# Test operations on paired words and on every second word of a bank, placed ahead of the first matmul

## What is computed

```python
h = rmsnorm(x, norm_g)
proj = jnp.einsum('bld,dn->bln', h, w_in)            # first layer, 18432 columns
...
ya = jnp.einsum('blc,cd->bld', ya * jax.nn.silu(za), w_out_a)
yb = jax.nn.gelu(s5_scan(u, a_re, a_im, log_dt, b_re, b_im, c_re, c_im, d_skip))
...
return x + jnp.einsum('bld,de->ble', m, w_o)
...
mod = cond @ w_ada[l] + b_ada[l]                     # second layer
h = rms_norm(x, norm_g[l]) * (1.0 + scale[:, None, :]) + shift[:, None, :]
z = h @ w_in[l]
...
y = jnp.concatenate([y_a, y_b], axis=-1) @ w_out[l]
x = x + gate[:, None, :] * y
return rms_norm(x, final_g)
```

## Time and profile before

| | us |
|---|---|
| median of 3 runs | 2667.97 |
| lowest and highest run | 2667.52, 2670.11 |
| the profiled execution's own time | 2670.03 |
| its span, first to last instruction | 2668.8 |

### The profile page before, as it was taken

The page is one execution under the profiler, slowest core; times in us unless marked ns, Lnnn a source line. Parts: engine busy times, 40 slices in busy tenths (PEclk is TensorE's granted clock), DMA queues, the critical chain, the costliest instruction groups (busy, mean ns, idle before and its releaser), DMA issues.

```text
span 2668.8 us, 30016 instructions
## 1 busy us (share of the span) xinstructions
PE 2631.5 (99%) x11928; PEld 2159.8 (81%) x11928; DVE 1638.4 (61%) x2187; ACT 845.1 (32%) x1139; POOL 390.9 (15%) x295
## 2 busy tenths in 40 slices
PE   9989999999999999999999999999999999999997
PEld 7878888888888888888888888877888888888786
DVE  6678888787887765445444775556465563234434
ACT  5122222222222222222322332332565563233321
POOL 0034343433443421000000000010000000000001
PEclk9999999999999999999999999989999999999999
DMA  5233333333333333667555675623222222322333
GB/s 184 96 112 112 105 114 99 121 110 104 116 103 125 128 121 120 215 202 245 186 193 192 207 240 181 197 95 129 95 80 73 86 80 87 111 95 87 115 122 111
DMA packets 119867, 353.07 MB, mean 132 GB/s; under 512 B 15408, under 2 KB 22832, under 8 KB 119728
## 3 DMA queue, kind: packets, MB, share of 16 engines
q1 hardware_dynamic: 119728, 351.16, 39.7%
HBM read 321.68 MB, written 23.07 MB: 129 GB/s over the span
## 4 chain that ended last, share of the span: by engine, by line
PE 96%; DVE 2%; issue 1%; POOL 0%; ACT 0%; DMA 0%; SPq 0%; DVEq 0%; POOLq 0%; ACTq 0%
PE bank L512 29%; PE bank L513 28%; PE bank L514 28%; PE bank L678 2%; PE bank L680 2%; PE bank L679 2%; PE bank L721 1%; PE bank L711 1%; PE bank L576 1%; PE bank L564 1%; DVE X L1814 0%; PE bank L704 0%; PE bank L702 0%; PE bank L502 0%; DMA W<-in_w 0%
## 5 line engine op out<-in xcount | busy, mean ns | idle before, releaser
L1138 DVE TENSOR_TENSOR WL<-W,WH 128x1024 fp32r<-128x1024 f32 (+1 forms) x456 | 592.2, 1301 | 528.3 <-ACT WH L816 527.0
L816 ACT ACTIVATE WH<-W 128x1024 fp32r<-128x1024 f32 (+1 forms) x456 | 480.6, 1056 | 1008.6 <-PE bank L514 768.8
L512 PE MATMUL bank<-hH,WH 128*128 128x512 f32 x1792 | 700.3, 391 | 10.7 <-DVE WL L1138 6.8
L513 PE MATMUL bank<-hL,WH 128*128 128x512 f32 x1792 | 699.1, 390 | 0.0
L514 PE MATMUL bank<-hH,WL 128*128 128x512 f32 x1792 | 698.8, 390 | 0.0
L512 PEld LDWEIGHTS bank<-hH,WH 128*128 128x128 f32 x1792 | 337.1, 188 | 89.9 <-DVE WL L1138 7.2
L514 PEld LDWEIGHTS bank<-hH,WL 128*128 128x128 f32 x1792 | 337.1, 188 | 70.6
L513 PEld LDWEIGHTS bank<-hL,WH 128*128 128x128 f32 x1792 | 337.2, 188 | 70.2
L512 PE MATMUL bank<-h2H,WH 128*128 128x512 f32 x640 | 252.6, 395 | 0.1
L514 PE MATMUL bank<-h2H,WL 128*128 128x512 f32 x640 | 249.4, 390 | 0.0
L513 PE MATMUL bank<-h2L,WH 128*128 128x512 f32 x640 | 249.1, 389 | 0.0
(11 more groups left out here) (260 smaller groups left out, 3604.5 us busy)
## 6 DMA issues: line engine op xcount, KB each, us to landing
W<-in_w SPq DMA_DIRECT2D x335, 512.0 KB, 3.7
W<-in_ada SPq DMA_DIRECT2D x96, 512.0 KB, 4.4
W<-in_wa SPq DMA_DIRECT2D x32, 512.0 KB, 3.9
W<-in_wo SPq DMA_DIRECT2D x32, 512.0 KB, 3.9
W<-in_wvv SPq DMA_DIRECT2D x32, 512.0 KB, 3.7
W<-in_wb SPq DMA_DIRECT2D x16, 512.0 KB, 3.7
URAW<-U SPq DMA_DIRECT2D x96, 64.0 KB, 3.1
scr_am<-SO SPq DMA_DIRECT2D x16, 256.0 KB, 2.0
```

Source lines behind the costliest of these rows:

```text
L512: e.matmul(o, wh, xh, start=first, stop=False)
L513: e.matmul(o, wh, xl, start=False, stop=False)
L816: e.activation(WH[:, n % NB, c], W[:, i % NW, c], ACT.Copy).then_inc(sem["hi"], 1)
L1138: e.tensor_tensor(WL[:, s, c], W[:, plan.item_of[n] % NW, c], WH[:, s, c].bitcast(F32), ALU.subtract).then_inc(sem["lo_v"], 1)
```

## The change

At the head of the program test operations are put in, whose results nothing reads. The 12 warm-up matmuls go.

GpSimd first fills four tiles with 0.5: `TM` (128x2048 words), `TW` (128x128), `TQ` and `TD[0]` (128x512 each). They lie in memory that is not in use at this time. TensorE waits for `const` and for the second and third of these signals, runs 14 matmuls of 512 columns in fp32r into banks 7 and 6, signals, and then runs 42 + 8 + 6 + 9 further ones in fp32r and 3 + 3 + 8 in f32, nearly all with a moving operand whose words are read in another order, and one on `IDT`, all into bank 5. When the 14 are through, VectorE runs 27 operations of 512 words on bank 7 and on `TD`, and ScalarE 18 of 256 words on bank 6 and on `TD[0]`; both wait after each for its own signal. VectorE's `keep_u(0)`, which writes over the test tiles for the first time, waits for the last test matmul and for ScalarE's tests.

```diff
+    TM, TW = at("TM", 164, [128, 2048], F32R), at("TW", 172, [128, 128], F32R)
+    TQ = at("TQ", 172.5, [128, 512])
+    TD = [at(f"TD{i}", 174.5 + 2 * i, [128, 512]) for i in range(2)]
+    TR = at("TR", 178.5, [128, 256], F32R)
...
         e.wait_ge(*nth("const", 4))
-        for _ in range(WARM):
-            e.matmul(bank[7][:, 0:128], IDT[:, :], IDT[:, :], start=True, stop=True)
+        e.wait_ge(*nth("test", 2))
+        for i in range(14):
+            mm = e.matmul(bank[7 - i % 2][:, :], TW[:, :], TM[:, 0:512], start=True, stop=True)
+        mm.then_inc(sem["test"], 1)
+        x = TM[:, 0:512]
+        two = x.rearrange("p (a b) -> p b a", a=2)
+        for m in (two,
+                  x.rearrange("p (b a) -> p b a", a=2),
+                  x.rearrange("p (a b) -> p b a", a=4),
+                  x.rearrange("p (c a b) -> p c b a", a=2, b=16),
+                  x.rearrange("p (c a b) -> p c b a", a=2, b=128),
+                  TM[:, :].rearrange("p (a b) -> p b a", a=2)[:, 0:256, :],
+                  x.rearrange("p (c a b) -> p c b a", a=4, b=64)):
+            for i in range(6):
+                e.matmul(bank[5][:, :], TW[:, :], m, start=True, stop=True)
+        for i in range(8):
+            e.matmul(bank[5][:, 0:256], TW[:, :], TM[:, 0:256].rearrange("p (a b) -> p b a", a=2), start=True, stop=True)
+        for i in range(6):
+            e.matmul(bank[5][:, :], TW[0:64, :], two[0:64], start=True, stop=True)
+        for i in range(9):
+            e.matmul(bank[5][:, :], TW[:, :], two, start=i == 0, stop=i == 8)
+        for i in range(3):
+            e.matmul(bank[5][:, :], TQ[:, 0:128], TQ[:, :], start=True, stop=True)
+        for i in range(3):
+            e.matmul(bank[5][:, :], TQ[:, 0:128], TQ[:, :].rearrange("p (a b) -> p b a", a=2), start=True, stop=True)
+        for m in (TQ[:, :], TQ[:, :].rearrange("p (a b) -> p b a", a=2)):
+            for i in range(2):
+                for r in range(2):
+                    e.matmul(bank[5][rows[r], :], TQ[:, 0:64], m, start=True, stop=True)
+        e.matmul(bank[5][:, 0:128], IDT[:, :], IDT[:, :], start=True, stop=True).then_inc(sem["test"], 1)
...
         root_table()
+        e.wait_ge(*nth("test", 3))
+        tok = lambda x: x.rearrange("p (b a) -> p a b", a=2)
+        blk = lambda x: x.rearrange("p (a b) -> p a b", a=2)
+        pair = lambda x: x.rearrange("p (a b) -> p b a", a=2)
+        nat = lambda x: x.rearrange("p (b a) -> p b a", a=2)
+        n_test = 0
+        for src in (bank[6][:, 0:256], TD[0][:, 0:256]):
+            for f, g in ((nat, nat), (tok, blk), (nat, pair)):
+                for _ in range(3):
+                    e.activation(g(TR[:, :]), f(src), ACT.Copy).then_inc(sem["test_a"], 1)
+                    n_test += 1
+                    e.wait_ge(sem["test_a"], n_test)
...
+        e.wait_ge(*nth("test", 3))
+        b7, b6 = bank[7][:, :], bank[6][:, :]
...
+        s, o = TD[0][:, :], TD[1][:, :]
+        for f, g in ((nat, nat), (tok, blk), (nat, pair)):
+            for _ in range(3):
+                step("test_v", e.tensor_tensor(g(o), f(b7), f(s) if g is pair else g(s), ALU.mult))
+            for _ in range(3):
+                step("test_v", e.tensor_tensor(g(o), f(s), f(s), ALU.mult))
+            for _ in range(3):
+                step("test_v", e.scalar_tensor_tensor(out=g(o), in0=f(b7), scalar=2.0, in1=g(s), op0=ALU.mult,
+                                                      op1=ALU.add))
         e.wait_ge(*nth("hi_first", 0))
...
+            if m == 0:
+                e.wait_ge(*nth("test", 4))
+                e.wait_ge(sem["test_a"], 18)
...
+        e.memset(TM[:, :].bitcast(F32), 0.5)
+        e.memset(TW[:, :].bitcast(F32), 0.5).then_inc(sem["test"], 1)
+        e.memset(TQ[:, :], 0.5).then_inc(sem["test"], 1)
+        e.memset(TD[0][:, :], 0.5).then_inc(sem["test"], 1)
         e.memset(ONE[:, :], 1.0).then_inc(sem["const"], 1)
```

More of the change, by code:

```diff
@@ L44 @@
 SIGNALS = {
-    "par": 1, "const": 1, "w_first": 16, "hi_first": 1, "lo_first": 1, "hi": 1, "lo_v": 1, "used": 1,
+    "test": 1, "test_v": 1, "test_a": 1, "par": 1, "const": 1, "w_first": 16, "hi_first": 1, "lo_first": 1, "hi": 1, "lo_v": 1, "used": 1,
     "xh": 1, "xl": 1, "xsq": 1, "xacc": 1, "silu_c": 1,
@@ L1126, in dve_program @@
         at_unit = [0]
-        at_step = {"prm_v": 0, "fg_v": 0, "rms_v": 0, "ln_v": 0, "n_v": 0}
+        at_step = {"prm_v": 0, "fg_v": 0, "rms_v": 0, "ln_v": 0, "n_v": 0, "test_v": 0}
         def step(name, ins):
```

## The result

The changed kernel takes 2692.16 us (median of 3 runs, 2691.7 to 2694.04) against 2667.97 us (2667.52 to 2670.11): 24.2 us more, a ratio of 1.009 with a 95% interval of 1.0067 to 1.0113. Run again beside the experiments it takes 2692.43 us against 2668.01 us, 24.4 us more (1.0076 to 1.0103). The forecast was 2697.5 us, with a range of 2689 to 2722; of the rivals, (4), where hops cost VectorE nothing, lies nearer, at 2689.8. One run of the kernel before, measured beside three of the experiments, took 4084.4 us at a mean granted clock of 0.606; the ratios leave it out, and the median of the 21 runs there, 2668.78 us, would be 0.1 us lower without it.

A forecast was written before the change was run, and what follows sets the result against it. TensorE, busy 99% of the span, was taken as the bound, so a later stream start adds in full. VectorE's tests end at 38.6 us, plus 1.4 and 1.4 gives 41.4; less 11.9, +29.5 us: 2697.5 us, range 2689 to 2722.

The forecast's parts named there:

- (4): Rival on VectorE's tests at the head: hops cost VectorE nothing; +21.8 us, 2689.8 us; chance 0.07.
- S - 11.9: Added time: S is when TensorE's gapless stream of triples can start, 41.4 us forecast, against 11.9 us before; +29.5 us.
- P: End of TensorE's tests at the head, forecast as 21.2 + 55 r us.
- D: End of VectorE's tests at the head, forecast at 38.6 us: 10.7 + 19.6 + 8.3.
- I take 0.46: VectorE's tests: each of 18 operations with hopping or every-second-word access costs 0.46 us extra, 8.3 us in all.
- The row of 32 words 32 apart: Profile row behind VectorE's hop price: 221 ns against 192 contiguous, so 0.9 ns a word, 0.46 us per 512.
- The row of pairs: Profile row for VectorE, two adjacent words then a hop: 64 words in 230 to 240 ns, read as no penalty.
- r: Unknown time of one hopping fp32r test matmul on TensorE, 0.2275 to 0.69 us; forecast holds up to 0.37.
- the five f32 rounds: TensorE's f32 tests that hop: 0.46 us more each would raise rival (2) from 2715.2 to 2717.5 us.
- rival (2): TensorE's tests pay per hopped word what VectorE pays, 0.69 us per matmul; +47.3 us, 2715.2 us; chance 0.17.
- (1): Rival: TensorE's tests end last, hops at half rate, 0.45 us a step; +34.1 us, 2702.1 us; chance 0.20.
- (3): Rival: hops cost TensorE twice VectorE's penalty, 1.15 us per matmul; +72.6 us, 2740.6 us; chance 0.10.

## Why the prediction was right, and what was off

**The frame held.** The change costs S - 11.9, with S the later of two ends. The fifth unit and the mark both moved by 24 us, nothing later took part, and the waits for `hL` fell from 3.9 to 1.0 us. With the two measured ends, P = 34.2 us (last test 33.96 plus its 0.24) and D = 33.07 us, the prediction's own sum gives the later of 34.2 and 33.07 + 2.8 = 35.9 us, so 24.0 us. That is what was measured. VectorE was last for the stream as a whole, as forecast, but by 1.7 us, where the forecast left room for 7.7 (41.4 against the 33.7 us of the lowest r). What was mis-sized are terms of the two ends.

**TensorE's start and the 14.** 4.8 us was forecast and 4.78 came. Their end was put at 10.4; it came at 9.58, and at 9.51 to 10.86 in the other runs. The forecast took twelve of them at the lower clock, as long as the warm-up had lasted; 14 in 4.80 us are eight at 0.43 and six at 0.23 us. How many are cold differs from one execution to the next, and the draw is 0.8 us of the miss.

**VectorE's tests: the mis-sized term.** "I take 0.46, since a single word with a gap behind it is nearer to the row of single words": this failed for every second word. It cost 0.03 us per operation in memory and nothing from a bank, so 9 x 0.46 = 4.1 us of the 8.3 never came. The hopping writes came 10.16 / 9 = 1.13 us apart (22.91 to 33.07 us), so they cost 1.13 - 0.725 = 0.40 us for the 0.46 taken, another 0.5 us. With the contiguous ones right (0.725 us), VectorE was through at 33.07 us where 38.6 was forecast: 5.5 us, of which 0.9 from its earlier start. The row of 32 words 32 apart was no measure for words 2 apart, written or read. For writes by turns it came near, 0.9 ns a word against 0.42 us / 512 = 0.8 ns; that was luck, since nothing said that a price at 32 words holds at 256, and for reads it does not. The row of pairs was also read too low: it shows 230 to 240 ns where 192 + 32 x 1.04 is 225; the sum does not use it.

**TensorE's tests: r.** Taken as unknown between 0.2275 and 0.69, it was near the lower end: (19.50 - 9.58) / 42 = 0.236 us on average in L625, a mix of 0.216, 0.227 and 0.28. P = 21.2 + 55 x 0.236 = 34.2 is where TensorE came out, but partly because two errors cancel: the 14 ended 0.8 us early, and hops cost the five f32 rounds (29.94 - 26.60) / 3 - (26.60 - 24.03) / 3 = 0.26 us each, 1.3 us that stood only in rival (2), of which 0.6 us came back because a round of f32 took 0.86 us contiguous where 0.92 was taken. A single order, two streams by turns, lies below the lower bound that I took for r, near the floor of 0.213 that I named.

**The rivals.** (1), (2) and (3) fell with r. (4) had VectorE at 30.3 and TensorE at 33.7 us; TensorE's end came near that of (4), and the time lies between (4) and the forecast, because the hopping writes do cost. Only (4) had its two ends this close, 0.6 us apart at S, and that the ends are close is why either engine's tests alone cost nearly the whole.

**The rule on lines of memory.** A read that goes to another line each time pays a penalty, the Trainium skill says (Advanced Engine Details and Errata, § SBUF Cachelines). For TensorE's two streams by turns the runs say the opposite, 0.216 against 0.227 us, at hops from 16 to 1024 words. Every second word, with two hits on each line of four words, is where it does pay, 0.451 us. The measurement decides.

## What to carry to other kernels

Put a price on an unseen access pattern per engine and per side, read or write, before it enters a sum; a row of another distance is no bound. Where two engines must both be ready, compute both ends: taking VectorE's tests away saved 2 us of 24, and taking TensorE's away saved nothing. In a kernel bound by fp32r matmuls of 512 columns, read the moving operand as two interleaved halves and let the readers of the bank take every second word: 4% here, for no added work.

## What the runs showed of the hardware

- fp32r matmuls of 512 columns come 0.2160 us apart when the moving operand alternates between two streams, and 0.2267 us when it is contiguous, in the real stream as with constant words. Why two streams are faster was not found.
- Four streams 0.28 us; every second or fourth word 0.45 to 0.46 us.
- VectorE pays 0.36 to 0.42 us per 512 words for a write by turns between two places 256 words apart, nothing for a read by turns, nothing for writing every second word, and nothing for reading every second word of a bank. For reading every second word of memory on both operands it paid 0, 0.03 and 0.16 us in three settings, the first with TensorE standing still.
- The granted clock is down to the lower of its two levels (0.50, 1.2 GHz) behind waits of 6.7 us and of 24 us, and not where 26 matmuls fill the wait. How long it stays down behind the same wait differs between executions, some 6 us in the profile of before and 3.5 us in that of after; the runs of each kernel lie up to 3.5 us apart.
- Between 2 and 7 us the windows print a granted clock of 1.00 while matmuls take the time of 1.2 GHz: at the head, the length of the records counts.
